# A feed-forward tile taken token block by token block, one unit of modulation steps moved behind the keys, and a changed order of modulation and residual sum

## What is computed

```python
mod = cond @ ada_w[i] + ada_b[i]                  # per layer: shift, scale, gate, twice
h = modulate(rms_norm(x, norm_mix[i]), sh_m, sc_m)
y = retention(h, ...)        # layer 0;   stick_breaking(h, k_sh, v_sh, ...) in layer 1
x = x + g_m * y
h = modulate(rms_norm(x, norm_ff[i]), sh_f, sc_f)
y = swiglu(h, ff_w_in, ff_w_out)                  # layer 0: (silu(a) * b) @ w_out, width 2816
y = moe_swiglu(h, ...)                            # layer 1: top 2 of 8 experts, width 3584
x = x + g_f * y
# after layer 0: hk = modulate(rms_norm(x, kv_norm), sh_kv, sc_kv); k_sh, v_sh = hk @ kv_w
```

## Time and profile before

| what | before |
|---|---|
| runs, us | 1580.38, 1581.42, 1585.17; median 1581.42 |
| profiled execution, us | 1584.38 |
| its span, first to last instruction, us | 1582.7 |
| busy, share of the span | PE 96%, PEld 80%, DVE 90%, ACT 68%, POOL 4% |
| mean granted TensorE clock | 0.990 |
| read from HBM | 499.28 MB, 316 GB/s over the span |
| chain that ended last | PE 78%, DVE 11%, issue 4%, DMA 4%, ACT 2% |

### The profile page before, as it was taken

How to read it: one execution, slowest core, us unless ns; L and a number is a source line. 1 busy time by engine, 2 the same in 40 slices (tenths; PEclk the granted TensorE clock), 3 DMA queues, 4 the chain that set the end, 5 groups by cost and what they waited for, 6 DMA issues and landing times.

```text
span 1582.7 us, 22661 instructions
## 1 busy us (share of the span) xinstructions
PE 1521.7 (96%) x7210; PEld 1261.4 (80%) x7210; DVE 1424.5 (90%) x1650; ACT 1071.9 (68%) x1239; POOL 60.3 (4%) x47
## 2 busy tenths in 40 slices
PE   5999997999989999999999999999999999999997
PEld 5788876888869878788888888888888888888875
DVE  6988999778888767899999999999999999999997
ACT  2544445444447555888788888878888887887875
POOL 0222300000000110000000000000000000000000
PEclk9999999999999998999999999999999999999999
DMA  9977676788867232899999999999999999999993
GB/s 323 348 281 273 250 273 233 264 309 304 295 232 264 103 115 102 313 384 391 350 380 387 372 356 387 383 360 378 392 361 363 391 378 357 381 393 347 376 370 141
DMA packets 235122, 500.98 MB, mean 317 GB/s; under 512 B 9745, under 2 KB 40641, under 8 KB 235073
## 3 DMA queue, kind: packets, MB, share of 16 engines
q1 hardware_dynamic: 233904, 500.29, 86.6%
q10 hardware_dynamic: 1168, 0.07, 0.1%
HBM read 499.28 MB, written 1.05 MB: 316 GB/s over the span
## 4 chain that ended last, share of the span: by engine, by line
PE 78%; DVE 11%; issue 4%; DMA 4%; ACT 2%; POOL 1%; DVEq 0%; SPq 0%; ACTq 0%; POOLq 0%
PE ps L535 21%; PE ps L537 21%; PE ps L536 21%; DVE w_lo L1750 3%; DVE acc L1769 3%; DMA ada<-in_ada_w 3%; PE ps L1044 1%; PE ps L1105 1%; PE ps L1045 1%; PE ps L823 1%; PE ps L825 1%; PE ps L827 1%; PE ps L1065 1%; PE ps L1067 1%; DMA raw<-in_ret_w_in 1%
## 5 line engine op out<-in xcount | busy, mean ns | idle before, releaser
L1750 DVE TENSOR_TENSOR w_lo<-raw,w_hi 128x1024 fp32r<-128x1024 f32 x834 | 988.3, 1230 | 47.7 <-ACT w_hi L1291 40.9
L1291 ACT ACTIVATE w_hi<-raw 128x1024 fp32r<-128x1024 f32 x834 | 850.9, 1056 | 191.2 <-PE ps L537 164.4
L535 PE MATMUL ps<-w_hi,RA 128*128 128x512 f32 x1360 | 540.3, 397 | 7.0 <-DVE w_lo L1750 3.4
L537 PE MATMUL ps<-w_hi,RA 128*128 128x512 f32 x1360 | 531.0, 390 | 0.0
L536 PE MATMUL ps<-w_lo,RA 128*128 128x512 f32 x1360 | 530.2, 390 | 0.0
L535 PEld LDWEIGHTS ps<-w_hi,RA 128*128 128x128 f32 x1360 | 255.9, 188 | 60.9 <-DVE w_lo L1750 5.6
L537 PEld LDWEIGHTS ps<-w_hi,RA 128*128 128x128 f32 x1360 | 255.7, 188 | 54.6
L536 PEld LDWEIGHTS ps<-w_lo,RA 128*128 128x128 f32 x1360 | 256.1, 188 | 51.4 <-issue 0.7
L535 PE MATMUL ps<-w_hi,hT_hi 128*128 128x512 f32 x400 | 160.4, 401 | 10.8 <-DVE hT_lo L1816 5.1
L537 PE MATMUL ps<-w_hi,hT_lo 128*128 128x512 f32 x400 | 157.1, 393 | 0.0
L536 PE MATMUL ps<-w_lo,hT_hi 128*128 128x512 f32 x400 | 157.0, 392 | 0.0
(11 more groups left out here) (324 smaller groups left out, 1258.3 us busy)
## 6 DMA issues: line engine op xcount, KB each, us to landing
raw<-in_moe_w_in SPq DMA_DIRECT2D x224, 1024.0 KB
raw<-in_moe_w_out SPq DMA_DIRECT2D x112, 1024.0 KB
ada<-in_ada_w SPq DMA_DIRECT2D x46, 1024.0 KB, 7.4
raw<-in_ff_w_in SPq DMA_DIRECT2D x44, 512.0 KB
raw<-in_ret_w_in SPq DMA_DIRECT2D x16, 1024.0 KB
raw<-in_ff_w_out SPq DMA_DIRECT2D x11, 1024.0 KB
raw<-in_ret_w_in SPq DMA_DIRECT2D x16, 512.0 KB
raw<-in_ret_w_out SPq DMA_DIRECT2D x8, 1024.0 KB
```

The costliest lines, as they stand in the source:

```text
L535: pe.matmul(out, a_hi, b_hi, start=first, stop=False)
L537: return pe.matmul(out, a_lo, b_hi, start=False, stop=last)
L1291: act.activation(w_hi[:, cn % RING, cols], raw[:, cn % RAW, cols], ACT.Copy).then_inc(hi_done, 1)
L1750: v.tensor_tensor(w_lo[:, cn % RING, cols], raw[:, cn % RAW, cols], w_hi[:, cn % RING, cols].bitcast(f32), ALU.subtract).then_inc(lo_done, 1)
```

## The change

Three things are done. The last feed-forward tile (j = 10) is taken by blocks: w_in product of block 0, w_out product of tile 9 for block 0, transposes of block 0, w_in product of block 1, last w_out product of block 0 (which sets `y_ok`), then the rest of block 1. `ff_last_act`, `ff_last_product`, `ff_last_T`, `ff_last_high` and `ff_last_low` are the old silu, product, transposes and splits on one block (128x256 instead of 128x512). The transposed block gets buffers of its own, `lT_hi` and `lT_lo`, in `RA`. Unit 23 of the modulation leaves the feed-forward layer: its steps now stand beside key quarters 9 to 13, where those of unit 24 were, its transposes behind `columns(U_KV + 4)`, and units 24 to 26 each move down, the last four steps of unit 26 behind `log_weights(7)`. VectorE modulates block 0 before it adds block 1. And the diagonal of the attention gate moves on GpSimd behind the last mask, its broadcast on TensorE from in front of `out_block(0, 0)` to behind it.

```diff
@@ sync
-            ada_after = {0: (22, 0), 1: (22, 1), 3: (23, 0), 4: (23, 1), 6: (24, 0), 8: (24, 1), 10: (25, 0), ...
+            ada_after = {0: (22, 0), 1: (22, 1), 3: (23, 0), 4: (23, 1), 7: (24, 0), 9: (24, 1), 10: (25, 0), ...
@@ gpsimd, in the loop over the pairs of heads and behind it
-                if c == 5:
-                    pool.wait_ge(ada_step, 27 * 8)
-                    diagonal(2, diag2, MIX1 + G, 21)
+            pool.wait_ge(ada_step, 27 * 8)
+            diagonal(2, diag2, MIX1 + G, 21)
@@ tensor
-            ff_two(0, 0)
-            with pe.Fori(0, 4) as k:
-                ff_two(k + 1, k + 1)
-            pe.wait_ge(fTl_ok, FT)
-            block_rows(U_FF + 32, fT_hi, fT_lo, 0, 0, 4, False, True).then_inc(y_ok, 1)
-            block_rows(U_FF + 32, fT_hi, fT_lo, 0, 1, 6, False, True)
-            pe.wait_ge(mod_ok, 23)
-            reduce_ada(23, 3)
-            transpose_x(2, 0)
+            for o in range(2):
+                ff_one(0, 0, o)
+            with pe.Fori(0, 3) as k:
+                for o in range(2):
+                    ff_one(k + 1, k + 1, o)
+            ff_one(4, 4, 0)
+            pe.wait_ge(fg_ok, FT - 1)
+            block_half(U_FF + 29, 0, 0, 0, 1)
+            block_half(U_FF + 29, 1, 0, 0, 1).then_inc(in0_done, 1)
+            pe.wait_ge(mod_ok, 22)
+            reduce_ada(22, 3)
+            pe.wait_ge(fTl_ok, FT - 1)
+            block_rows(U_FF + 31, fT_hi, fT_lo, 0, 0, 4, False, False)
+            ff_last_T(0)
+            block_half(U_FF + 29, 0, 1, 1, 1)
+            block_half(U_FF + 29, 1, 1, 1, 1)
+            pe.wait_ge(Tbl_ok, 1)
+            block_rows(U_FF + 32, lT_hi, lT_lo, 0, 0, 4, False, True).then_inc(y_ok, 1)
+            ff_last_T(1)
+            block_rows(U_FF + 31, fT_hi, fT_lo, 0, 1, 6, False, False)
+            pe.wait_ge(Tbl_ok, 2)
+            block_rows(U_FF + 32, lT_hi, lT_lo, 0, 1, 6, False, True)
+            transpose_x(2, 0)
...
             columns(U_KV + 4, 0, 4, 4, 3, hq_hi, hq_lo)
+            reduce_last(23)
             pe.wait_ge(kq_ev, 1)
             columns(U_KV + 6, 0, 1, 6, 2, hT_hi, hT_lo)
             scores(0)
...
             mix_values(7)
-            broadcast_gate(2, diag2, 2)
             pe.wait_ge(ol_ok, KC)
             out_block(0, 0)
+            broadcast_gate(2, diag2, 2)
             out_block(0, 1).then_inc(y_ok, 1)
@@ scalar
+            ff_one(0, 4)
+            split_quarters(U_FF + 31, 0, 1, 2)
+            act.wait_ge(in0_done, 1)
+            ff_last_act(0)
+            ff_last_high(0)
+            split_quarters(U_FF + 31, 0, 2, 4)
+            act.wait_ge(w_used, before_half(U_FF + 31))
+            ff_last_act(1)
+            split_quarters(U_KV, 0, 0, 2)
+            ff_last_high(1)
             root_table()
             root_mean_square(2, 0)
-            split_quarters(U_KV, 0, 4, 5)
+            split_quarters(U_KV, 0, 2, 5)
             modulate(2, 2, 0, KVM + SH, U_KV - 2)
@@ vector
+            ff_one(0, 4)
+            split_quarters(U_FF + 31, 0, 1, 2)
+            ff_last_product(0)
+            ff_last_low(0)
+            mod_out(22, 3)
+            split_quarters(U_FF + 31, 0, 2, 4)
+            ff_last_product(1)
             scale_col(2, KVM + SC, V_KVN, 15)
             scale_col(3, MIX1 + SC, V_MIX + KC, 19)
             add_gated(1, 0, gate_f, f_tmp)
+            ff_last_low(1)
+            split_quarters(U_KV, 0, 0, 2)
+            normed(2, 0)
+            modulate(2, 2, 0, KVM + SH)
+            add_gated(1, 1, gate_f, f_tmp)
+            split_quarters(U_KV, 0, 2, 3)
+            normed(2, 1)
             split_quarters(U_KV, 0, 3, 4)
-            normed(2, 0)
-            mod_out(23, 3)
-            add_gated(1, 1, gate_f, f_tmp)
-            modulate(2, 2, 0, KVM + SH)
-            split_quarters(U_KV, 0, 4, 5)
-            normed(2, 1)
-            split_quarters(U_KV, 0, 5, 6)
             modulate(2, 2, 1, KVM + SH)
+            split_quarters(U_KV, 0, 4, 6)
...
-            woven(U_KV, 0, (9, 14), 24, (0, 8))
-            woven(U_KV, 0, (14, 18), 25, (0, 4))
+            woven(U_KV, 0, (9, 14), 23, (0, 8))
+            woven(U_KV, 0, (14, 16), 24, (0, 4))
+            mod_last(23)
+            woven(U_KV, 0, (16, 18), 24, (4, 8))
...
             log_weights(7)
+            ada_steps(26, 4, 8)
             split_quarters(U_MOE, 0, 0, 1)
```

More of the change, by code:

```diff
@@ L148, in trunk @@
         fT_lo = ra(512, 2, S)
+        lT_hi = ra(1024, 2, S)
+        lT_lo = ra(1536, 2, S)
         v_all = fa(0, NB, D)
@@ L665, in block_half @@
                         last.then_inc(w_used, 1)
+                return last
             def tile_by_blocks(c, banks, q):
@@ L802, in _, with ff_one @@
-            pe.wait_ge(fTl_ok, FT)
-            block_rows(U_FF + 32, fT_hi, fT_lo, 0, 0, 4, False, True).then_inc(y_ok, 1)
-            block_rows(U_FF + 32, fT_hi, fT_lo, 0, 1, 6, False, True)
+            def ff_one(i, m, o):
+                c = U_FF + 2 + 3 * o
+                ff_in(c, m, 2 * i + (1 + o))
+                pe.wait_ge(mod_ok, 2 * i + (13 + o))
+                reduce_ada(13 + o, 3, i)
+                ff_out(c + 2, m, 2 * i + o, isinstance(i, int) and i == 0 and o == 0, False)
+                ff_T(2 * i + (1 + o))
@@ new lines, in ff_last_T @@
+            def ff_last_T(b):
+                pe.wait_ge(gb_ok, b + 1)
+                for c in range(2):
+                    last = pe.transpose(ps[:, 2, c * S + b * P:c * S + (b + 1) * P], f_g[:, b, c * P:(c + 1) * P],
+                                        ident[:, :])
+                last.then_inc(Tb_done, 1)
+            for o in range(2):
+                ff_one(0, 0, o)
+            with pe.Fori(0, 3) as k:
+                for o in range(2):
+                    ff_one(k + 1, k + 1, o)
@@ L1998, in _, with ff_one, ff_last_product, ff_last_low @@
             split_quarters(U_FF + 2, 0, 4, 5)
-            def ff_two(i):
-                for o in range(2):
[L2003 to L2014, removed]
+            def ff_one(o, i):
+                c, j = U_FF + 2 + 3 * o, 2 * i + (1 + o)
+                woven(c, i, (5, 8), 14 + o, (0, 4), i)
+                ff_product(j)
+                mod_out(13 + o, 3, i)
+                woven(c, i, (8, 11), 14 + o, (4, 6), i)
+                ff_low(j)
+                ada_steps(14 + o, 6, 8, i)
+            def ff_last_product(b):
+                dve.wait_ge(sab_ok, b + 1)
+                v.tensor_tensor(f_g[:, b, :], ps[:, b, FW:2 * FW], f_sa[:, b, :], ALU.mult).then_inc(gb_ok, 1)
+            def ff_last_low(b):
+                dve.wait_ge(Tbh_ok, b + 1)
+                tok = slice(b * P, (b + 1) * P)
+                v.tensor_tensor(lT_lo[:, :, tok], ps[:, 2, :].rearrange("p (c s) -> p c s", c=2)[:, :, tok],
+                                lT_hi[:, :, tok].bitcast(f32), ALU.subtract).then_inc(Tbl_ok, 1)
+            with dve.Fori(0, 4) as k:
+                steps.enter(k, 2)
+                for o in range(2):
+                    ff_one(o, k)
+                steps.leave(4)
+            ff_one(0, 4)
+            split_quarters(U_FF + 31, 0, 1, 2)
+            dve.wait_ge(fT_done, FT - 1)
+            ff_last_product(0)
[3 more added lines that the diff above has]
+            ff_last_product(1)
             scale_col(2, KVM + SC, V_KVN, 15)
@@ L2077, in _ @@
             log_weights(0)
-            ada_steps(25, 4, 5)
+            ada_steps(25, 0, 1)
             quarter(21)
             log_weights(1)
-            ada_steps(25, 5, 7)
+            ada_steps(25, 1, 3)
             softplus(2)
@@ L2090, in _ @@
             log_weights(3)
-            ada_steps(25, 7, 8)
-            ada_steps(26, 0, 2)
+            ada_steps(25, 3, 6)
             low_o(2)
@@ L2095, in _ @@
             low_o(3)
-            ada_steps(26, 2, 4)
+            ada_steps(25, 6, 8)
             softplus(4)
             quarter(26)
-            ada_steps(26, 4, 5)
+            ada_steps(26, 0, 1)
             softplus(5)
@@ L2102, in _ @@
             log_weights(4)
-            ada_steps(26, 5, 7)
+            ada_steps(26, 1, 3)
             quarter(28)
             log_weights(5)
-            ada_steps(26, 7, 8)
+            ada_steps(26, 3, 4)
             softplus(6)
```

39 lines of the change are left out of this document (21 added, 18 removed).

## The result

| | median, us | lowest to highest | runs |
|---|---|---|---|
| before | 1581.25 | 1578.26 to 1585.56 | 22 |
| after | 1584.43 | 1581.14 to 1587.11 | 22 |

The ratio is 1.0015, with a 95% interval of 1.0008 to 1.0021: some 2.4 us slower, where 2.9 us faster was forecast. The median of 1584.43 lies above the forecast range, which ended at 1583.7.

What follows compares the result with a forecast made beforehand. TensorE is busy throughout the experts, so time it wins ahead of them was taken to move the end. 4.1 - 2.6 + 3.5 - 2.1 = 2.9 us faster gave a median of 1578.5 us, range 1574.5 to 1583.7.

Steps and rivals of the forecast that it cites:

- moved unit: At the keys, TensorE waits 2 us for unit 24's steps behind the first scores; 1.5 us of the lead is left.
- lead of the join: Between feed-forward layer and keys: block 1 can start at 471.1 instead of 475.2, 4.1 us earlier.
- diagonal: At the last tails: idle time ahead of `softplus(7)` shrinks to 0.7 us, slow clock goes; 3.5 us gained, bounds 1.7 and 4.1.
- broadcast: At the attention gate: TensorE waits 1.0 us and block 0's gated sum comes 2.8 later; 2.1 us lost, bounds 1.0 and 2.8.
- The feed-forward tile by blocks: Last feed-forward tile: TensorE's reordered matmuls take 17.2 us up to `y_ok`, so block 0's sum starts at 451.9 instead of 456.56.
- The sum and the norm: Block 0 ahead of the keys: TensorE starts on the keys' unit at 461.85 instead of 466.71, 4.9 us earlier.
- Where part of it goes back: Block 1 comes late: TensorE waits 2.8 us ahead of its transposes, clock at full speed; the lead becomes 4.1 us.
- rival 3: The clock falls in the join when block 1's transposes run: lead 2.1, total 0.9 us faster, 1580.5; chance 0.20.
- Its DMAs: Transfers of unit 24 at the keys: first half just in time, second lands at 506.4, 0.2 us late, bounds 505.1 and 507.9.
- Rival 1: Second DMA half 1.5 us late, TensorE waits 3.6, slow clock follows; 2.2 us slower in all, 1583.6; chance 0.15.

Runs made afterwards that it cites:

- e2: e1 with diagonal and gate broadcast also back at their old places, so only the tile by blocks and the modulation order are left; 0.9983 to before.
- e1: After with unit 23's steps and reduce back in the last feed-forward tile and the keys' side as before; 0.9981 to before.
- e5: e1 with the broadcast in front of `out_block(0, 0)` again and the diagonal still late; 0.9966 to before.
- e8: e2 with VectorE's old order, block 1's sum ahead of block 0's modulation; 0.9977 to before.
- e11: e5 with VectorE's old order, block 1's sum ahead of block 0's modulation; 0.9973 to before.
- e4: After with the DMAs of key units 41 and 42 issued ahead of both halves of unit 24; 1.0005 to before.
- e6: After with unit 24's reduce moved from behind the first scores to behind the second, `mod_last(24)` behind `softplus(0)`; 0.9970 to before.
- e9: e6 with the broadcast in front of `out_block(0, 0)` again; 0.9959 to before, 1574.66 against 1582.36 us.
- e10: e9 with the DMAs of key units 41 and 42 ahead of unit 24's, as in e4; 0.9956 to before.
- e12: After with the last feed-forward tile whole again and the old order on VectorE; unit 23 stays at the keys, the gate late; 1.0030 to before.
- e7: Before with only VectorE's modulation of block 0 moved ahead of its sum of block 1; 0.9995 to before.
- e3: Before with only the gate edits: diagonal behind the last mask, broadcast behind `out_block(0, 0)`; 1.0005 to before.

## Why the prediction was wrong

The step that failed is TensorE's wait for the moved unit. The prediction put it at 2 us with no slow clock behind it. It measured 4.0, and the half clock behind it cost 2.5 more.

The forecast was 4.1 - 2.6 + 3.5 - 2.1 = 2.9 faster. The runs give 2.7 (e2) - 5.4 (after against e1) + 2.7 (e5 against e2) - 2.4 (e5 against e1) = -2.4, thus slower. That this is the measured ratio of after proves nothing: in this sum e1, e2 and e5 cancel. The terms stand by their own pairs of runs.

| term | forecast, us | measured by ratios | by traces |
|---|---|---|---|
| lead of the join | +4.1 | +2.7 (0.6 to 4.7) | after +4.4; unit 23 back: e2 +4.2, e1 +2.5, e5 +2.6, e8 and e11 +2.7 |
| moved unit | -2.6 | -5.4 (-7.3 to -3.6) | -6.7 from after's lead, -5.0 against e1 |
| diagonal | +3.5 | +2.7 (-0.1 to 5.5), second pair +0.6 (-1.7 to 2.9) | +2.9 to +3.0, to the gated sum |
| broadcast | -2.1 | -2.4 (-4.9 to 0.1), second pair -1.7 (-4.5 to 1.0) | -3.0, to the gated sum |

**The feed-forward tile by blocks, right.** The sum of block 0 was to start at 451.9. It starts at 450.49 + 1.46 = 451.95. The order of matmuls, counted by their spacings, gave the place to 0.1 us.

**The sum and the norm, right.** The keys' first matmul was forecast for 461.85, measured 461.67.

**Where part of it goes back, right in size, not in its reason.** I put TensorE's wait for block 1 at 2.8 and the clock at full speed. In after the clock was at half for block 0's matmuls, from 460.0 to 463.4, so the wait was only 0.95; the slow clock ran inside time that would have been idle and cost nothing. In e5 the first matmuls were fast, and the clock fell behind the wait, in the transposes:

```profile
467.32 1.32 PE L585 MATMUL ps<-ident,FA 128*128 128x128 f32 x8 [2.86 <-DVE FA L1851]
```

Its first modulation step at the keys is 51.1 from the mark, so its lead is 53.7 - 51.1 = 2.6. This is rival 3's mechanism, and it can explain why the ratios give less than after's trace. Of the five traces with unit 23 back, four have a lead of 2.5 to 2.7, as the ratios have it, and only e2, whose clock fell in block 0's matmuls, has 4.2. With the unit at the keys the clock fell there in all five traces of the new tile (after, e4, e6, e9, e10), behind a wait of 2.62, and the lead was 4.4 or more. So the departure of the unit's steps, for which the prediction booked nothing, may win some 1.5 us here. It is one trace each, and no run isolates it.

**The unit that is moved: the step that failed.** I wrote that TensorE "waits 2". The first half of that working holds: TensorE reaches the reduce 20.1 us behind quarter 9 (502.26 against 482.13), and the prediction's places give 20.2. But unit 24 is complete 24.1 behind it, not 22.1. Of the 2.0 missing, 1.3 are the second DMA half, 1.5 late where **Its DMAs** had put 0.2, at the upper end of its own bounds; the rest lies in small gaps that I did not trace one by one. And the sum left out what follows such a wait. I had the row for it: an idle 2.37 was followed by the slow clock. With a wait of 2 the sum took no drop. At 4.0 it came and cost 2.5. It came as well behind 3.9 in e12, 2.4 in e4 and 1.7 in e6, so it belonged in the sum even at the wait that I forecast. Four transposes more, the wait and the drop are 0.5 + 4.0 + 2.5 = 7.0; the trace has 6.7 lost. The 5.4 of the ratios is another difference, that between after and e1, and e1 starts the keys with 1.9 less lead than after. At the last decline after is 5.0 behind e1 (137.1 from the mark, against 132.1), which agrees.

Rival 1 had just this: a second half 1.5 late, a wait of 3.6, a slow clock behind it. Its point of decision, unit 24 complete later than 507.7, was met only to the rounding: 506.22 + 1.46 = 507.68. What I had named in its favour, VectorE full from 488 to 504, was the larger part of the cause: by e4, which has no late transfer, VectorE's list alone leaves a wait of 2.4. Its 2.2 slower against 2.4 measured is partly luck: the idle stretch at the last tails did not bring the slow clock, as it assumed, and the ratios have a lead of 2.7 and not 4.1. Its chance of 0.15 was too little.

**The diagonal, right in mechanism.** The clock stayed at 1.00 through 579, as forecast, and the idle stretch of 2.37 shrank to 0.68. The two quarters at 570.92 took 2.35 together, for 4.05 in the earlier trace rows. After's rows of VectorE, TensorE and GpSimd:

```profile
570.92 2.35 DVE L1799 TENSOR_TENSOR w_lo<-raw,w_hi 128x1024 fp32r<-128x1024 f32 x2
...
577.33 0.70 PE L913 MATMUL ps<-FA,after 128*128 128x256 f32 x2 [0.68 <-DVE FA L2130]
...
584.35 1.90 POOL L490 TENSOR_TENSOR ada<-ident,modc 128x1024 f32<-128x1024 f32 x1 [1.42 <-DVE acc L1818]
```

All four traces with the diagonal at its old place (before, e2, e7, e8) have the stretch of 2.36 or so and half clock behind it, and none of the ten others has either. The gain in time is less certain: the two pairs of runs, with 2.7 and 0.6, both lie under the forecast of 3.5, and neither is clear of nothing. Its price at the new place is seen at 584.62: a `w_lo` of 2.71, 1.49 over the usual 1.22, beside a diagonal with 1.63 left to run (584.35 + 1.90 - 584.62). In before, 1.70 over, with 570.18 - 568.35 = 1.83 left. The Trainium skill's rule (SBUF — State Buffer, section Who interferes with whom), that the second stops fully until the first is done, fits both rows to within 0.14 us once one counts from the second's start. I had counted the diagonal's whole 2.4, which made the rule look wrong by 0.7; it was my count. At the gated sum this price hardly shows: after is 26.38 behind the last decline, and e1, where the diagonal is done ahead of that quarter, 26.28.

**The broadcast, right in mechanism.** I took 2.1, with 2.8 at the sum. The sum came 3.0 late, and the two pairs of runs give 2.4 and 1.7. The reason is the one given: ScalarE's gate copy, at 592.82, and the quarter behind it stand ahead of VectorE's sum in strict lists.

## What to carry to other kernels

Work that is moved from a hidden place to one where a strict list waits for it has to be priced by both queues from a common start: what each does until the meeting point, the transfers behind their neighbours in the queue included. If the difference is a few us, move the meeting point, not the work: one `reduce` placed some 4 us of matmuls later won back 7 us without removing anything. A wait of some 2 us or more on TensorE is to be booked with the half clock that may follow (1.7 and 2.5 us here). Two edits at one place should be looked at apart, or one hides the other: here +2.9 and -3.0 by the traces, and nothing together in e3.

## What the hardware did that I had not expected

The same idle stretch of 1.9 us, at `mix_values(3)`, left the granted clock alone in before and was followed by half clock in e1. Windows of before and then of e1 (columns as above):

```profile
544.00:545.00 1.00, 1.00 (x9) 0.76 (x10) 1.00 (x3) 0.77 (x2) 0.00 (x0) 1.00 0.83 285
```

```profile
540.00:541.00 1.00, 1.00 (x4) 0.71 (x4) 0.96 (x2) 0.00 (x0) 0.00 (x0) 0.50 1.05 395
```

In after the stretch was 2.3 us, and the clock 0.50 at 546. Over all fourteen traces, the stretch at this place was 1.9 us in eight, of which three were followed by half clock (e1, e2, e7), and 2.3 us in five, of which again three were (after, e6, e10, but not e4 and e12). In e9 it was 1.65, and the clock stayed up. At `reduce_last(24)` all four waits of 1.7 to 4.0 were followed by it, and so were all four of 2.36 at the last tails. So whether a stretch of about 2 us is followed by a drop changes from trace to trace at one place and not at another, and each drop costs 1.7 us or more where TensorE is busy.

I take this for one source of the 7 us between the lowest and the highest run of before. The recorded clocks point that way. Of the 22 runs of after, the four with a mean granted clock of 0.991 are the four fastest (1581.1 to 1581.9), and three of the four with 0.984 are the three slowest (1586.6 to 1587.1). No run isolates it. A gain of 3 us could not be read from one profiled execution, but only from repeated runs.
